# The expert loop of a hybrid encoder layer: silu's table load outside the loop, down's parts split at a slot's head, weight parts signalled in halves

## The chip, the cores and the metric

One core of a Trainium2 chip runs the whole kernel. The metric is the device time of one execution in microseconds (us). Times of this kernel are medians over several executions; a profile is one execution of its own, read by its span, which runs from the first to the last instruction.

## What is computed

The layer takes 1024 tokens of width 1024 in float32. It mixes them with two kinds of attention, then with attention over a memory of 256 tokens, and then routes them through 16 experts, of which each token uses two. The change touches only the last step:

```python
moe = jnp.zeros_like(t)
for e in range(N_EXPERTS):
    he = jax.nn.silu(t @ w_gate[e]) * (t @ w_up[e])
    moe = moe + gates[:, e:e + 1] * (he @ w_down[e])
h = h + moe.reshape(B, S, D)
```

`w_gate[e]` and `w_up[e]` are 1024 x 512, `w_down[e]` is 512 x 1024, all float32, 2 MB each.

## The kernel before

Each engine has an instruction stream of its own, written by hand, and they meet at semaphores (`wait_ge`, `then_inc`). The order of the work is the order in which each stream is written; no scheduler changes it.

**Slots.** Routing sorts the 2048 pairs of token and expert into slots of up to 128 rows of one expert. The number of slots depends on the data; in the run shown it is 24. Each engine runs one loop over them (`Fori(0, n_slots)`). An expert with more than 128 rows has two slots in a row; a table `newt` says for each slot whether its expert is another than the last one's.

**Split products.** A float32 product is made of three products of rounded parts: high x high, high x rest and rest x high (`split_product`, L1792). So each weight part must be split. ACT copies the loaded buffer `stage[part]` to `split[part][0]`, the high part (`high`, L1070), and DVE subtracts that from the loaded one, which gives the rest part (`rest`, L1455). Part 0 is gate, 1 is up, 2 is down. Each is split in four steps of 128 x 1024 elements (`PARTS = 4`), and ACT signals every step. The split is repeated in a slot that keeps its expert, but the load is skipped. There is one loaded buffer, one high and one rest buffer for each part.

**PE in slot s** (L2182 on). It multiplies the slot's rows by gate (24 matmuls into bank 2), then by up in two halves of the columns (24 + 24, banks 3 and 4), turns the first half of the product `hrow` (L2195), turns the rows of the next slot (`rows_in`, L2168), turns the second half of `hrow`, and multiplies by down (24 matmuls, banks 6 and 7). Before each weight part it waits with `weights` until DVE has signalled the whole rest part.

**ACT in slot s** (L1171 on). It waits for the gate product and applies silu (L1174), splits gate of the next slot, copies the turned `hrow` and the rows of the next slot (L1178, L1161), splits up of the next slot, waits for the down product and copies it out (L1186, the sum copies), and splits down of the next slot.

**DVE in slot s** (L1730 on). It does gate rest steps 0 and 1 of the next slot, then `hrow` = silu x share x up for the first half (L1737), gate step 2, `hrow` for the second half, the rest parts of `hrow` and of the next rows (L1744, L1719), gate step 3, and all of up and down of the next slot.

**SP** (L648 on) issues the loads. The load of a part for slot s + 2 waits until the rest of that part for slot s + 1 is done, and the order is gate, up, down. An issue whose expert stays moves nothing. **POOL** (L743 on) gathers the rows of a later slot once `rows_in` has emptied the buffer (L729), and adds the result rows to the output in HBM (L733) once ACT has copied them out.

Of the kernel before, what the change touches and what calls it, by code (L numbers as in the profile page):

```python
# [40 lines left out]
PARTS = 4  # L41
# [110 lines left out]
def moe_layer(nc, x, mem, positions, norm_mix_g, w_in, mla_q_norm_g, w_uq, mla_kv_norm_g, w_ukv,  # L152
# [18 lines left out]
    with ctx:  # L171
# [333 lines left out]
        def bank(i):  # L505
            return psum[:, i, :]
# [17 lines left out]
        def _(sp):  # L524
# [123 lines left out]
            def next_weights(s, parts, e, new):  # L648
                for part in parts:

                    sp.wait_ge(s_lo[part], s)
                    load(e, part, new > 0)
# [5 lines left out]
            next_weights(1, range(3), *plan(1))  # L658
            last = sp.snap(n_slots - 1)
            with sp.Fori(0, last) as s:  # L660
                e, new = plan(s + 2)
                next_weights(s + 2, range(3), e, new)
# [7 lines left out]
        def _(pool):  # L670
# [85 lines left out]
            all_split = pool.snap(n_slots + 1)  # L756
# [6 lines left out]
        def _(act):  # L763
# [298 lines left out]
            def high(s, part, used):  # L1062

                n = (DC if part < 2 else FC) // PARTS
                act.wait_ge(s_st[part], 16 * s + 16)
                if used is not None:
                    act.wait_ge(used, s)
                for c in range(PARTS):
                    k = slice(n * c, n * c + n)
                    act.activation(split[part][0][:, k, :], stage[part][:, k, :], ACT.Copy).then_inc(s_hi[part], 1)  # L1070
# [95 lines left out]
            high(0, 2, None)  # L1166
            act.wait_ge(s_ys, FIRST_ROWS)
            rows_high(0)
            act.wait_ge(s_plan, 1)
            n_slots = act.value_load(ends_i[0:1, NE - 1:NE], min_val=NE, max_val=SLOTS - 1)  # L1170
            with act.Fori(0, n_slots) as s:  # L1171

                act.wait_ge(s_gf, s + 1)
                act.activation(hrow, bank(2), ACT.Silu).then_inc(s_si, 1)  # L1174
                high(s + 1, 0, s_gf)
                for half in range(2):
                    act.wait_ge(s_ht, 2 * s + 1 + half)
                    act.activation(hTe[0][:, 2 * half:2 * half + 2, :].rearrange("p a b -> p (a b)"),  # L1178
                                   bank(5 - 2 * half)[:, 0:2 * P], ACT.Copy).then_inc(s_hth, 1)
                    if half == 0:  # L1180
                        rows_high(s + 1)
                high(s + 1, 1, s_ub)
                act.wait_ge(s_y, s + 1)
                act.wait_ge(s_yf, s + 1)
                for half in range(2):
                    act.activation(ysb[:, 512 * half:512 * half + 512], bank(6 + half), ACT.Copy).then_inc(s_yo, 1)  # L1186
                high(s + 1, 2, s_y)
# [3 lines left out]
        def _(dve):  # L1191
# [257 lines left out]
            def rest(s, part, steps):  # L1449

                n = (DC if part < 2 else FC) // PARTS
                for c in steps:
# [4 lines left out]
                    if c == PARTS - 1:  # L1457
                        ins.then_inc(s_lo[part], 1)
# [269 lines left out]
            rest(0, 2, range(PARTS))  # L1728
            n_slots = dve.value_load(ends_i[0:1, NE - 1:NE], min_val=NE, max_val=SLOTS - 1)
            with dve.Fori(0, n_slots) as s:  # L1730
                rest(s + 1, 0, (0, 1))
                for half, full in enumerate((s_ua, s_ub)):
                    cols = slice(256 * half, 256 * half + 256)
                    if half == 0:
                        dve.wait_ge(s_si, s + 1)
# [3 lines left out]
                    if half == 0:  # L1739
                        rest(s + 1, 0, (2,))  # L1740
# [7 lines left out]
                rest(s + 1, 0, (3,))  # L1748
                rest(s + 1, 1, range(PARTS))
                rest(s + 1, 2, range(PARTS))  # L1750
# [3 lines left out]
        def _(pe):  # L1754
# [416 lines left out]
            def weights(s, part):  # L2171

                pe.wait_ge(s_lo[part], s + 1)
# [8 lines left out]
            with pe.Fori(0, n_slots) as s:  # L2182
                pe.wait_ge(s_xl, 2 * s + 2)
                weights(s, 0)
                rows = lambda a, k: xT[a][:, k, :]
                split_product(bank(2), DC, rows, lambda b, k: split[0][b][:, k, :], s_gf)
                weights(s, 1)
                for half, full in enumerate((s_ua, s_ub)):
                    cols = slice(256 * half, 256 * half + 256)
                    split_product(bank(3 + half)[:, 0:256], DC, rows, lambda b, k: split[1][b][:, k, cols], full)  # L2190
# [8 lines left out]
                weights(s, 2)  # L2199
                for part in range(2):  # L2200
                    pe.wait_ge(s_htl, 2 * s + 1 + part)
# [33 lines left out]
```

## Time and profile before

| | us |
|---|---|
| median of 3 runs | 1583.45 |
| lowest and highest run | 1582.7, 1586.78 |
| the profiled execution's own time | 1585.15 |
| its span | 1583.4 |
| mean granted TensorE clock, share of full speed | 0.963 |

The page of the profile gives each engine's busy time as a share of the span. The windows give the same for chosen stretches. The list of waits groups idle time by the instruction that ended it. A timeline row has a start, a duration, the engine, the line and the operation with its output and inputs, how many instructions were merged, and in brackets how long the engine was idle before it and what released it. PEld is TensorE's loading of weights, which overlaps the matmuls. SPq is SP issuing a DMA.

### The profile page before, as it was taken

The page shows a single profiled execution, that of the slowest core. Times are in us where ns is not written, and L with a number is a line of the kernel's source. Part 1 is how long each engine was busy: PE and PEld are TensorE (multiplying, and loading weights), DVE is VectorE, ACT ScalarE, POOL GpSimd, SP SyncE. Part 2 cuts the span into 40 slices and gives each one's busy share as a digit, 9 for nine tenths or more (in the row PEclk, how much of TensorE's full clock was granted, in tenths as well). Part 3 has the DMA queues.
Part 4 walks back from the last instruction along what each step waited for, and adds up shares of the span by engine and source line. Part 5 has one row for each costly group of instructions (what it writes and reads, how often), then busy time and mean ns, then how long its engine had stood idle before and what let it go on. Part 6 is the DMA issues. An engine that isn't in the chain of part 4 may idle for free.

```text
span 1583.4 us, 20901 instructions
## 1 busy us (share of the span) xinstructions
PE 1453.7 (92%) x7417; PEld 1112.8 (70%) x7417; DVE 1030.1 (65%) x1900; ACT 925.7 (58%) x1624; POOL 167.5 (11%) x243
## 2 busy tenths in 40 slices
PE   6999999987889689999989999996999999999996
PEld 5888988444446444447868888885888888788885
DVE  4512126689759667757773333448888888888887
ACT  6320556676756545663333333343888888888886
POOL 0000000356610000000000000000111111111111
PEclk9999999999999789999989999996999999999998
DMA  6210215310020000102130100044996666666693
GB/s 213 57 34 8 96 68 213 143 47 1 1 107 1 1 1 28 54 27 84 50 120 1 54 28 27 28 160 161 372 360 215 202 207 204 202 205 212 212 366 102
DMA packets 87300, 184.81 MB, mean 117 GB/s; under 512 B 14273, under 2 KB 24513, under 8 KB 86465
## 3 DMA queue, kind: packets, MB, share of 16 engines
q1 hardware_dynamic: 77952, 161.90, 28.5%
q0 software_dynamic: 7200, 22.03, 5.4%
q8 instruction: 39, 0.64, 0.2%
q10 hardware_dynamic: 2080, 0.01, 0.1%
q14 instruction: 29, 0.23, 0.0%
HBM read 218.52 MB, written 26.21 MB: 155 GB/s over the span
## 4 chain that ended last, share of the span: by engine, by line
PE 63%; DMA 12%; DVE 9%; ACT 8%; issue 6%; POOL 1%; DVEq 0%; ACTq 0%; SPq 0%; POOLq 0%
PE psum L1792 21%; PE psum L2023 17%; DMA down_stage<-in_w_down 10%; PE psum L1776 7%; PE psum L1919 6%; PE psum L1940 4%; PE psum L1769 3%; PE psum L1906 3%; DVE down_rest L1455 3%; ACT down_high L1070 2%; POOL arena L709 1%; DVE gate_rest L1455 1%; DVE mx L1418 1%; PE psum L2072 1%; ACT L1174 1%
## 5 line engine op out<-in xcount | busy, mean ns | idle before, releaser
L1919 PE MATMUL psum<-arena 64*128 64x512 f32 (+7 forms) x384 | 124.1, 545 | 20.6 <-ACT arena L1041 12.0
L1455 DVE TENSOR_TENSOR gate_rest<-gate_stage,gate_high 128x1024 fp32r<-128x1024 f32 x100 | 119.8, 1220 | 31.3 <-ACT gate_high L1070 31.3
L1455 DVE TENSOR_TENSOR down_rest<-down_stage,down_high 128x1024 fp32r<-128x1024 f32 x100 | 115.8, 1220 | 31.1 <-ACT down_high L1070 31.1
L1919 PEld LDWEIGHTS psum<-arena 64*128 64x128 f32 (+1 forms) x384 | 50.2, 196 | 102.0 <-issue 46.9
L1455 DVE TENSOR_TENSOR up_rest<-up_stage,up_high 128x1024 fp32r<-128x1024 f32 x100 | 115.8, 1220 | 7.7 <-ACT up_high L1070 7.5
L1776 PE MATMUL psum<-arena 128*128 128x512 f32 (+2 forms) x352 | 119.2, 491 | 0.8 <-DVE arena L1361 0.8
L1940 PEld LDWEIGHTS psum<-ident,arena 128*128 128x128 f32 x576 | 70.8, 152 | 66.6 <-ACT arena L774 32.7
L774 ACT ACTIVATE arena<-psum 128x512 f32<-128x512 f32 (+1 forms) x192 | 85.8, 501 | 49.2 <-PE psum L1940 49.1
L1940 PE MATMUL psum<-ident,arena 128*128 128x128 f32 x576 | 93.6, 302 | 20.4 <-DVE arena L1377 14.3
L1792 PE MATMUL psum<-up_rest,rows_high 128*128 128x256 f32 x384 | 108.7, 283 | 0.0
L1070 ACT ACTIVATE up_high<-up_stage 128x1024 fp32r<-128x1024 f32 x100 | 97.5, 1049 | 19.0 <-DMA up_stage<-in_w_up 19.0
L1792 PE MATMUL psum<-up_high,rows_rest 128*128 128x256 f32 x384 | 108.6, 283 | 0.0
L1792 PE MATMUL psum<-up_high,rows_high 128*128 128x256 f32 x384 | 108.5, 283 | 0.0
L1369 DVE TENSOR_TENSOR_SCAN arena<-arena,singles 128x768 f32<-128x768 f32 (+7 forms) x64 | 90.9, 1420 | 27.0 <-POOL arena L709 26.9
L1070 ACT ACTIVATE down_high<-down_stage 128x1024 fp32r<-128x1024 f32 x100 | 97.6, 1053 | 17.0 <-DMA down_stage<-in_w_down 17.0
L709 POOL TENSOR_SCALAR_AFFINE_SELECT arena<-arena 128x128 f32<-128x128 f32 x128 | 94.5, 760 | 76.2 <-ACT arena L946 69.7
L1769 PE MATMUL psum<-ident,arena 128*128 128x128 f32 (+1 forms) x520 | 75.1, 287 | 28.9 <-ACT arena L791 12.5
L1070 ACT ACTIVATE gate_high<-gate_stage 128x1024 fp32r<-128x1024 f32 x100 | 97.3, 1048 | 5.4 <-DMA gate_stage<-in_w_gate 5.2
L1776 PEld LDWEIGHTS psum<-arena 128*128 128x128 f32 x352 | 66.0, 193 | 43.1 <-issue 26.7
L1769 PEld LDWEIGHTS psum<-ident,arena 128*128 128x128 f32 (+1 forms) x520 | 62.2, 143 | 44.6 <-issue 21.6
L1906 PE MATMUL psum<-arena 128*64 128x512 f32 (+3 forms) x384 | 84.8, 521 | 1.8 <-ACT arena L774 1.8
L1792 PE MATMUL psum<-down_high,hidden_high 128*128 128x512 f32 x192 | 77.6, 404 | 0.0
(362 smaller groups left out, 3649.0 us busy)
## 6 DMA issues: line engine op xcount, KB each, us to landing
gate_stage<-in_w_gate SPq DMA_DIRECT2D x25, 2048.0 KB
up_stage<-in_w_up SPq DMA_DIRECT2D x25, 2048.0 KB
down_stage<-in_w_down SPq DMA_DIRECT2D x25, 2048.0 KB
arena<-in_x SPq DMA_DIRECT2D x16, 512.0 KB, 3.6
arena<-in_w_mkv SPq DMA_DIRECT2D x8, 1024.0 KB, 6.2
arena<-in_w_in SPq DMA_DIRECT2D x4, 1024.0 KB, 10.1
arena<-in_w_mo SPq DMA_DIRECT2D x4, 1024.0 KB, 6.5
mv_times_w_mo_spill<-arena SPq DMA_DIRECT2D x8, 512.0 KB, 2.8
```

The costliest lines, as they stand in the source:

```text
L709: pool.affine_select(out=block_, in_=block_, compare_op=ALU.is_gt, fill=fill, base=0, pattern=[[-1, P]], channel_multiplier=1).then_inc(ma ...
L774: do(act.activation(dst, src, ACT.Copy), s_te["act"])
L1070: act.activation(split[part][0][:, k, :], stage[part][:, k, :], ACT.Copy).then_inc(s_hi[part], 1)
L1369: one(dve.tensor_tensor_scan(fall[:, a, SEQ - L:SEQ][:, ::-1], f_sb[:, n % 3, 0:L][:, ::-1], tiny.to_broadcast([P, L]), 1.0, ALU.mult, ALU ...
L1455: ins = dve.tensor_tensor(split[part][1][:, k, :], stage[part][:, k, :], split[part][0][:, k, :].bitcast(F32), ALU.subtract)
L1769: mm = pe.transpose(dst[0:rows, at:at + P], src, ident[:, :])
L1776: mm = pe.matmul(dst, a, b, start=(i == 0), stop=(i == n - 1))
L1792: mm = pe.matmul(dst, lhs(a, k), rhs(b, k), start=(k == 0 and i == 0), stop=(k == n - 1 and i == 2))
L1906: pe.matmul(bank(6 + u % 2)[HD * a:HD * a + HD, lo:512], value(p, a, j), bufs[:, k % 4, lo:512], start=(j == 0), stop=(j == GRP * g + 3)). ...
L1919: mm = pe.matmul(pair(1 + a)[:, at:end], lhs, rhs(at, end), start=True, stop=True)
L1940: mm = pe.transpose(dst[:, r * P:(r + 1) * P], rows(u, r, a)[:, j * P:(j + 1) * P], ident[:, :])
L2023: mm = pe.matmul(dst, lhs[a][:, k, :], w[b][:, k, cols], start=(k == ks[0] and k % n == 0 and i == 0), stop=(k % n == n - 1 and i == 2))
```

## The change

Before the loop ACT applies silu to one column, and no longer splits down for slot 0; nor does DVE. In the loop:

- ACT splits down of the present slot right behind silu, gate of the next slot behind the hidden and row parts, then step 0 of up, then the two sum copies, then up's steps 1 to 3.
- DVE does down step 0, the first half of `hrow`, down steps 1 and 2, the second half, the parts of `hrow` and rows, down step 3, and then all of gate and up of the next slot.
- DVE signals a rest part after its second and its fourth step, so that each count is double. PE waits for the first half before the first half of a product's matmuls and for the second half before the others. The number and order of the matmuls stay.
- SP issues down of slot s + 1 once down of slot s is split, and then gate and up of slot s + 2. The table of experts is read twice in an iteration.

```diff
@@ -645,21 +645,24 @@
             sp.wait_ge(s_plan, 1)
             n_slots = sp.value_load(ends_i[0:1, NE - 1:NE], min_val=NE, max_val=SLOTS - 1)
 
-            def next_weights(s, parts, e, new):
-                for part in parts:
-
-                    sp.wait_ge(s_lo[part], s)
-                    load(e, part, new > 0)
+            def next_weights(part, rests_done, e, new):
+                sp.wait_ge(s_lo[part], rests_done)
+                load(e, part, new > 0)
 
             def plan(s):
                 return (sp.value_load(eidt[0:1, bass.ds(s, 1)], min_val=0, max_val=NE - 1),
                         sp.value_load(newt[0:1, bass.ds(s, 1)], min_val=0, max_val=1))
 
-            next_weights(1, range(3), *plan(1))
+            e, new = plan(1)
+            for part in range(2):
+                next_weights(part, 2, e, new)
             last = sp.snap(n_slots - 1)
             with sp.Fori(0, last) as s:
+                e, new = plan(s + 1)
+                next_weights(2, 2 * s + 2, e, new)
                 e, new = plan(s + 2)
-                next_weights(s + 2, range(3), e, new)
+                for part in range(2):
+                    next_weights(part, 2 * s + 4, e, new)
             all_added = sp.snap(16 * n_slots)
             sp.wait_ge(s_ya, all_added)
             sp.sem_inc(s_end, 1)
@@ -753,7 +756,7 @@
                 pool.wait_ge(s_ya, 16 * s + 16)
                 pool.sem_inc(s_yf, 1)
             all_fetched = pool.snap(16 * n_slots + 32)
-            all_split = pool.snap(n_slots + 1)
+            all_split = pool.snap(2 * n_slots + 2)
             for part in range(2):
                 pool.wait_ge(s_lo[part], all_split)
             pool.wait_ge(s_xg, all_fetched)
@@ -1059,13 +1062,13 @@
                                   ACT.Square, scale=DM ** -0.5, accum_out=to), sem_)
                 do.settle()
 
-            def high(s, part, used):
+            def high(s, part, used, steps=range(PARTS)):
 
                 n = (DC if part < 2 else FC) // PARTS
                 act.wait_ge(s_st[part], 16 * s + 16)
                 if used is not None:
                     act.wait_ge(used, s)
-                for c in range(PARTS):
+                for c in steps:
                     k = slice(n * c, n * c + n)
                     act.activation(split[part][0][:, k, :], stage[part][:, k, :], ACT.Copy).then_inc(s_hi[part], 1)
 
@@ -1163,28 +1166,30 @@
 
             act.wait_ge(s_mop, T)
             high(0, 1, None)
-            high(0, 2, None)
             act.wait_ge(s_ys, FIRST_ROWS)
             rows_high(0)
+
+            do(act.activation(m4[:, 0:1], m4[:, 0:1], ACT.Silu))
             act.wait_ge(s_plan, 1)
             n_slots = act.value_load(ends_i[0:1, NE - 1:NE], min_val=NE, max_val=SLOTS - 1)
             with act.Fori(0, n_slots) as s:
 
                 act.wait_ge(s_gf, s + 1)
                 act.activation(hrow, bank(2), ACT.Silu).then_inc(s_si, 1)
-                high(s + 1, 0, s_gf)
+                high(s, 2, None)
                 for half in range(2):
                     act.wait_ge(s_ht, 2 * s + 1 + half)
                     act.activation(hTe[0][:, 2 * half:2 * half + 2, :].rearrange("p a b -> p (a b)"),
                                    bank(5 - 2 * half)[:, 0:2 * P], ACT.Copy).then_inc(s_hth, 1)
                     if half == 0:
                         rows_high(s + 1)
-                high(s + 1, 1, s_ub)
+                high(s + 1, 0, s_gf)
+                high(s + 1, 1, s_ub, (0,))
                 act.wait_ge(s_y, s + 1)
                 act.wait_ge(s_yf, s + 1)
                 for half in range(2):
                     act.activation(ysb[:, 512 * half:512 * half + 512], bank(6 + half), ACT.Copy).then_inc(s_yo, 1)
-                high(s + 1, 2, s_y)
+                high(s + 1, 1, None, (1, 2, 3))
 
 
         @block.vector
@@ -1454,7 +1459,7 @@
                     dve.wait_ge(s_hi[part], PARTS * s + c + 1)
                     ins = dve.tensor_tensor(split[part][1][:, k, :], stage[part][:, k, :],
                                             split[part][0][:, k, :].bitcast(F32), ALU.subtract)
-                    if c == PARTS - 1:
+                    if c % 2:
                         ins.then_inc(s_lo[part], 1)
 
             def tile_of(j):
@@ -1725,19 +1730,16 @@
             one(dve.tensor_copy(share, bank(7)[:, 0:TAB]))
             one(dve.tensor_tensor(share, share, bank(7)[:, TAB:2 * TAB], ALU.add))
             rest(0, 1, (1, 2, 3))
-            rest(0, 2, range(PARTS))
             n_slots = dve.value_load(ends_i[0:1, NE - 1:NE], min_val=NE, max_val=SLOTS - 1)
             with dve.Fori(0, n_slots) as s:
-                rest(s + 1, 0, (0, 1))
                 for half, full in enumerate((s_ua, s_ub)):
                     cols = slice(256 * half, 256 * half + 256)
+                    rest(s, 2, (1, 2) if half else (0,))
                     if half == 0:
                         dve.wait_ge(s_si, s + 1)
                     dve.wait_ge(full, s + 1)
                     dve.scalar_tensor_tensor(out=hrow[:, cols], in0=hrow[:, cols], scalar=share[:, bass.ds(s, 1)],
                                              in1=bank(3 + half)[:, 0:256], op0=ALU.mult, op1=ALU.mult).then_inc(s_h, 1)
-                    if half == 0:
-                        rest(s + 1, 0, (2,))
                 for half in range(2):
                     v = slice(2 * half, 2 * half + 2)
                     dve.wait_ge(s_hth, 2 * s + 1 + half)
@@ -1745,9 +1747,9 @@
                                       hTe[0][:, v, :].bitcast(F32), ALU.subtract).then_inc(s_htl, 1)
                     if half == 0:
                         rows_rest(s + 1)
-                rest(s + 1, 0, (3,))
+                rest(s, 2, (3,))
+                rest(s + 1, 0, range(PARTS))
                 rest(s + 1, 1, range(PARTS))
-                rest(s + 1, 2, range(PARTS))
 
 
         @block.tensor
@@ -2168,9 +2170,9 @@
                         mm = pe.transpose(bank(half)[:, c * P:(c + 1) * P], xg[:, at:at + P], ident[:, :])
                     mm.then_inc(s_xt, 1)
 
-            def weights(s, part):
-
-                pe.wait_ge(s_lo[part], s + 1)
+            def weights(s, part, half):
+
+                pe.wait_ge(s_lo[part], 2 * s + half + 1)
 
             pe.wait_ge(s_sh, 1)
             share_table(range(10))
@@ -2181,13 +2183,18 @@
             n_slots = pe.value_load(ends_i[0:1, NE - 1:NE], min_val=NE, max_val=SLOTS - 1)
             with pe.Fori(0, n_slots) as s:
                 pe.wait_ge(s_xl, 2 * s + 2)
-                weights(s, 0)
                 rows = lambda a, k: xT[a][:, k, :]
-                split_product(bank(2), DC, rows, lambda b, k: split[0][b][:, k, :], s_gf)
-                weights(s, 1)
+                for part in range(2):
+                    weights(s, 0, part)
+                    split_product(bank(2), DC, rows, lambda b, k: split[0][b][:, k, :], s_gf if part else None,
+                                  range(4 * part, 4 * part + 4))
                 for half, full in enumerate((s_ua, s_ub)):
                     cols = slice(256 * half, 256 * half + 256)
-                    split_product(bank(3 + half)[:, 0:256], DC, rows, lambda b, k: split[1][b][:, k, cols], full)
+                    for part in range(2):
+                        if half == 0:
+                            weights(s, 1, part)
+                        split_product(bank(3 + half)[:, 0:256], DC, rows, lambda b, k: split[1][b][:, k, cols],
+                                      full if part else None, range(4 * part, 4 * part + 4))
                 for half in range(2):
                     pe.wait_ge(s_h, 2 * s + 1 + half)
                     for c in range(2):
@@ -2196,8 +2203,8 @@
                     mm.then_inc(s_ht, 1)
                     if half == 0:
                         rows_in(s + 1)
-                weights(s, 2)
                 for part in range(2):
+                    weights(s, 2, part)
                     pe.wait_ge(s_htl, 2 * s + 1 + part)
                     for half in range(2):
                         split_product(bank(6 + half), FC, lambda a, k: hTe[a][:, k, :],
```

In the order of the built program the head of ACT's loop stood like this (the row `arena<-psum` at L1174 is silu):

```order
L1171 ISA
L1174 ACT_TABLE_LOAD
L1174 ACTIVATE arena<-psum 128x512
L1065 ISA
L1070 ACTIVATE gate_high<-gate_stage 128x1024 x4
```

and now, from just ahead of the loop (L1175 is its head, and silu is at L1178):

```order
L1164 ACTIVATE rows_high<-psum 128x512 x2
L1172 ACT_TABLE_LOAD
L1172 ACTIVATE m<-m 128x1
L1174 TENSOR_LOAD ends_i
L1174 ISA x2
L1175 UNCONDITIONAL_BRANCH
L1175 ISA
L1178 ACTIVATE arena<-psum 128x512
L1068 ISA
L1073 ACTIVATE down_high<-down_stage 128x1024 x4
```

The table load stands ahead of the loop, and down's high steps follow silu where gate's did.

The end of ACT's loop before, from the second hidden part on (`arena<-psum` x2 are the sum copies):

```order
L1178 ACTIVATE hidden_high<-psum 128x256
L1070 ACTIVATE up_high<-up_stage 128x1024 x4
L1186 ACTIVATE arena<-psum 128x512 x2
L1070 ACTIVATE down_high<-down_stage 128x1024 x4
L1171 REGISTER_ALU
```

and now:

```order
L1182 ACTIVATE hidden_high<-psum 128x256
L1068 ISA
L1073 ACTIVATE gate_high<-gate_stage 128x1024 x4
L1073 ACTIVATE up_high<-up_stage 128x1024
L1191 ACTIVATE arena<-psum 128x512 x2
L1073 ACTIVATE up_high<-up_stage 128x1024 x3
L1175 REGISTER_ALU
```

Gate's four steps and one of up's stand ahead of the sum copies now, and up's other three behind them.

The end of DVE's loop before, from the second hidden rest part on:

```order
L1744 TENSOR_TENSOR hidden_rest<-psum,hidden_high 128x256
L1454 REGISTER_ALU
L1455 TENSOR_TENSOR gate_rest<-gate_stage,gate_high 128x1024
L1455 TENSOR_TENSOR up_rest<-up_stage,up_high 128x1024 x4
L1455 TENSOR_TENSOR down_rest<-down_stage,down_high 128x1024 x4
```

and now:

```order
L1746 TENSOR_TENSOR hidden_rest<-psum,hidden_high 128x256
L1459 REGISTER_ALU
L1460 TENSOR_TENSOR down_rest<-down_stage,down_high 128x1024
L1459 ISA
L1460 TENSOR_TENSOR gate_rest<-gate_stage,gate_high 128x1024
L1459 REGISTER_ALU
L1460 TENSOR_TENSOR gate_rest<-gate_stage,gate_high 128x1024
L1459 REGISTER_ALU
L1460 TENSOR_TENSOR gate_rest<-gate_stage,gate_high 128x1024
L1459 REGISTER_ALU
L1460 TENSOR_TENSOR gate_rest<-gate_stage,gate_high 128x1024
L1460 TENSOR_TENSOR up_rest<-up_stage,up_high 128x1024 x4
```

Five steps stand between the hidden rest part and up's steps, where one stood.

## Rows read from the trace of the kernel before

**Rows 1.** The page, busy us of each engine, share of the span, instructions.

```profile
PE 1453.7 (92%) x7417; PEld 1112.8 (70%) x7417; DVE 1030.1 (65%) x1900; ACT 925.7 (58%) x1624; POOL 167.5 (11%) x243
```

**Rows 2.** Windows of the expert loop: length, busy us, clock, DMA share, GB/s.

```profile
1100.92:1120.91 19.99, 19.99 (x108) 17.26 (x109) 18.57 (x21) 10.76 (x14) 1.15 (x2) 0.92 1.00 371
1120.91:1218.56 97.65, 93.14 (x542) 80.56 (x540) 82.86 (x91) 81.53 (x100) 13.93 (x15) 1.00 0.88 305
1218.56:1530.53 311.97, 298.14 (x1729) 257.69 (x1728) 264.31 (x289) 259.63 (x320) 44.41 (x48) 1.00 0.67 225
1530.53:1569.65 39.12, 37.66 (x217) 32.04 (x215) 33.15 (x37) 32.72 (x40) 5.55 (x6) 1.00 0.61 204
1257.81:1276.18 18.37, 18.37 (x109) 16.10 (x108) 15.57 (x18) 15.56 (x20) 2.77 (x3) 1.00 1.03 355
1276.18:1296.46 20.28, 18.75 (x110) 16.11 (x108) 17.49 (x20) 16.81 (x21) 2.78 (x3) 1.00 0.26 71
```

**Rows 3.** Waits in the loop: us in total, times, longest us.

```profile
PEld psum L2195 <- DVE arena L1737: 27.1, 33, 2.8
PE psum L2195 <- DVE arena L1737: 19.6, 29, 2.6
...
PE psum L1792 <- DVE rows_rest L1719: 0.4, 1, 0.4
...
ACT up_high L1070 <- DMA up_stage<-in_w_up: 19.0, 12, 2.0
```

**Rows 4.** Timeline of PE, the slot from 1257.81, and the next one's wait.

```profile
1263.29 0.28 PE L1792 MATMUL psum<-up_high,rows_high 128*128 128x256 f32 x1
...
1269.04 0.38 PE L2195 MATMUL psum<-ident,arena 128*128 128x128 f32 x2
...
1270.53 0.47 PE L1792 MATMUL psum<-down_high,hidden_high 128*128 128x512 f32 x1
...
1288.85 0.44 PE L2195 MATMUL psum<-ident,arena 128*128 128x128 f32 x2 [1.32 <-DVE arena L1737]
```

**Rows 5.** Timeline of ACT over the same two slots.

```profile
1272.90 3.91 ACT L1070 ACTIVATE up_high<-up_stage 128x1024 fp32r<-128x1024 f32 x4 [1.64 <-DMA up_stage<-in_w_up]
...
1279.25 3.90 ACT L1070 ACTIVATE down_high<-down_stage 128x1024 fp32r<-128x1024 f32 x4 [1.47 <-DMA down_stage<-in_w_down]
1283.17 1.28 ACT L1174 ACT_TABLE_LOAD   x1
1284.47 0.60 ACT L1174 ACTIVATE arena<-psum 128x512 f32<-128x512 f32 x1
```

**Rows 6.** Timeline of SP, issues of loads.

```profile
1109.20 0.37 SPq L539 DMA_DIRECT2D down_stage<-in_w_down  x1
...
1254.99 0.39 SPq L539 DMA_DIRECT2D gate_stage<-in_w_gate  x1
1259.22 0.38 SPq L539 DMA_DIRECT2D up_stage<-in_w_up  x1
...
1273.61 0.09 SPq L539 DMA_DIRECT2D gate_stage<-in_w_gate  x1
```

**Rows 7.** Timeline of DVE, the end of the row parts in the slot from 1257.81.

```profile
1271.73 0.41 DVE L1744 TENSOR_TENSOR hidden_rest<-psum,hidden_high 128x256 fp32r<-128x256 f32 x1
1272.07 1.22 DVE L1455 TENSOR_TENSOR gate_rest<-gate_stage,gate_high 128x1024 fp32r<-128x1024 f32 x1
1273.99 4.63 DVE L1455 TENSOR_TENSOR up_rest<-up_stage,up_high 128x1024 fp32r<-128x1024 f32 x4 [0.71 <-ACT up_high L1070]
```

**Rows 8.** Timeline of POOL, the issue of the adding DMA.

```profile
1260.00 1.59 POOL L733 DMA_INDIRECT layer_out<-arena,idx  x1 [6.31 <-ACT arena L1186]
```

**Rows 9.** Windows of DMA while gate, up and down land (columns as Rows 2).

```profile
1258.00:1265.00 7.00, 7.00 (x39) 6.02 (x39) 5.83 (x6) 6.96 (x9) 1.59 (x1) 1.00 1.02 363
1265.00:1269.00 4.00, 4.00 (x36) 4.00 (x35) 3.23 (x4) 3.58 (x4) 0.00 (x0) 1.00 1.04 244
...
1276.00:1278.00 2.00, 2.00 (x11) 1.65 (x9) 2.00 (x3) 1.78 (x3) 0.00 (x0) 1.00 0.92 365
```

## The prediction

> **What bounds the kernel now.** The page comes first. PE is busy 92% of the span and DVE 65%, but those are averages over stages with different limits [rows 1]. The change touches only the expert loop, so the table of windows is cut at its slots [rows 2]. The loop runs from 1100.92 to 1569.65 us, 468.7 us in 24 slots. A slot in which PE never waits takes 18.37 us, 1257.81 to 1276.18, with PE busy through all of it. The next one takes 20.28. Both are the same 24 gate, 48 up and 24 down matmuls, so every slot above 18.37 holds a wait (the first also runs at a granted clock of 0.92). The three stretches after it hold 97.65 - 5 x 18.37 = 5.8 us, 311.97 - 16 x 18.37 = 18.1 us and 39.12 - 2 x 18.37 = 2.4 us of excess, 26.3 us in all. That is the most that any reordering here can bring.
>
> The list of waits says where the excess sits [rows 3]: PE's weight loads wait 27.1 us for DVE's product `hrow` before its transposes (L2195), the matmuls themselves 19.6 us. That list has one other wait of PE in the loop, 0.4 us, and none for weight parts, so signalling parts in halves has nothing to win by itself. PE's timeline shows one such wait, 1.32 us at 1288.85 [rows 4]. Why `hrow` is late stands in ACT's timeline [rows 5]. In the slot before, `up_high` waits 1.64 us for its load, then `down_high` 1.47 us; after it come the table load, 1.28 us, and silu only at 1284.47. DVE does two gate steps and the product behind that. So DMA is late first and the table load makes it worse. DMA's share agrees [rows 2]: 1.03 at 355 GB/s in the slot from 1257.81, 0.26 in the next. SP's issues show why [rows 6]: an issue of 0.38 us is a real load, one of 0.09 is skipped because the expert stays. The first six slots each need a new expert, then every second, and both of the last two.
>
> **The change, part by part.** The sum is made against the profiled execution, 1585.15 us with a span of 1583.4. The median of the runs, 1583.45, is 1.7 lower, and I add the difference to it.
>
> The table load leaves the loop: 24 x 1.28 = 31 us less on ACT. The one that stays runs before the first gate product ends, while ACT waits: 0. It shortens the path only where ACT was late, 12 slots by the waits on up's load [rows 3], so at most 15 us, and only if nothing else is late there. The trace has silu 0.02 us behind the end of the load (1283.17 + 1.28, [rows 5]). The Trainium skill (ScalarE: Activation LUTs, section What ACT_TABLE_LOAD costs) adds 1.38 us of drain to a load. By the page those 12 slots would hold up to 17 us more for this cut; the trace shows no such gap, and the sum goes without it.
>
> ACT and DVE get the same weight work in another order. I lay a slot out from T, the start of its gate product, with the free slot's T = 1257.81. PE starts up at T+5.48, the transposes at T+11.23, down at T+12.72 [rows 4]. ACT: silu at T+5.7, four down steps of 0.96 (a group of four takes 3.90, [rows 5]) to T+10.0, the hidden and row parts behind the transposes, four gate steps from about T+13.7, up step 0 from T+17.5, the two sum copies, up steps 1 to 3 to T+22.5. It is free before the next silu at T+24.0. DVE's row parts end at T+14.3, where `gate_rest` follows now [rows 7]. With 1.135 a step (a group of four takes 4.63) down step 3 ends at T+15.5, the gate steps at T+20.0, the up steps at T+24.5. PE wants the second half of down at T+12.72+2.83 = T+15.55, up's two halves at T+23.85 and T+25.3. So without late loads a slot stays at 18.37, but one margin is under 0.1 us. The waits on halves are needed in this order: a whole gate part, ready at T+20.0 against T+18.37, would hold every slot 1.6 us.
>
> Loads move, since each waits for the rest steps that free its buffer. After the row parts DVE had one gate step to do, and a gate issue followed at 1273.61 = T+15.8 [rows 6]. Now one down and four gate steps stand there, four more, 4.5 us: T+20.3, which is 1.9 after the next T, where it was 2.8 before it (1254.99). Up goes by the same 4.5 from T+1.4 (1259.22) to about T+6.4, down to T+15.8. SP's two extra table reads and its new down wait stand between down's and gate's rest steps, 4.5 us apart, and cost nothing. Gate's high part moves from T+6.9 to T+13.7, further than its load. Up's moves from about T+13.1 to T+17.5, only as far as its load.
>
> So up's landing decides. From gate's issue to up's landing it took 17.9 us (1254.99 to 1272.90, [rows 5, 6]). In that DMA moved the two loads at 363 GB/s, and the added rows, whose DMA POOL issues at T+2.2, cut the rate to 244 GB/s for 4 us [rows 8, 9]. That issue stays at T+2.2, inside. The gather of the next rows fell into down's time before, around 1276 to 1278; now the end of up's load stands there. For it the floor is nothing and the ceiling is the 2 us of that window; I take 1.4, since down, which met it, was the load that ended there. Up lands at T + 1.9 + 17.9 + 1.4 = T+21.2, bounds T+19.8 and T+21.8.
>
> What PE loses from a landing at u: step 0 takes 0.96 and the sum copies 0.98, so step 1 ends at u+3.0. DVE then runs three steps of 1.135 and signals the last half at u+6.5. PE wants it at T+25.3. Above u = T+18.8 it waits one for one: 2.4 us at T+21.2, 1.0 and 3.0 at the bounds. Before, such a pair of slots lost 18.1/8 = 2.26. The wait changes its place, from the transposes to the up product, and hardly its size.
>
> Sum by stretch [rows 2]. First slot: 0. Slots 2 to 6: DMA carries an expert a slot, 371 GB/s at share 1.00 while it does, and the bytes stay. Down's second load goes some 9 us later (1109.20 to about 1118.3, the first T + 15.8 and the 1.6 us by which that slot is slow), a hole in DMA that the first slots' early loads mostly cover: +0.5, bounds -2 and +3. Slots 7 to 22: 8 x (2.4 - 2.26) = +1.1, bounds -10 and +6. Last two, both with new experts: +0.9, bounds -1 and +2. After the last product stand the same copies and the same adding DMA: 0. The sum is +2.5 us: **1583.45 + 2.5 = 1586.0**. A measurement of this kernel can tell 0.3%, 4.75 us, from no change, so this is a forecast of no change.
>
> **Rivals.**
> **A, the loads are covered, faster.** If up lands by T+18.8, the 18.1 us of slots 7 to 22 go: 1583.45 - 18 = 1565.5. At the lower bound of the landing 10 go: 1573.5. For it: DMA has a slot at share 0.26 behind each busy one, down's load now starts late and alone, and ACT has 1.28 us more. Against: the 17.9 us held only two loads and the adding DMA, with share 1.02 and 1.04 through it [rows 9]. 24 in 100.
>
> The Trainium skill (DMA: Bandwidth & Descriptors, section Bandwidth) measures 425 GB/s for the largest transfers. By that two loads of 2.1 MB take 1.6 us less than at 363 GB/s, up lands near T+19.6 and the time is about 1572. Rows 9 do not bear it out for gate and up.
>
> **B, the load falls deeper, slower.** Gather and adding DMA both fall wholly on up, and late sum copies push the next adding DMA into the following load. The point is u = T+21.5: there a pair loses 2.7, and 8 x 0.44 + 1.4 passes 4.75. Typical is u = T+22.1, 3.3 a pair: 8 x 1.04 + 1.4 = +9.7, 1593. For it: my landing is 0.3 us under that point, and the hole in the first slots. Against: the loads of the sole new expert have the next slot free. 22 in 100.
>
> **C, DVE becomes the bound, slower.** Down's last half has under 0.1 us to spare, and DVE's loop gets more register instructions and signals. From 0.2 us a slot on (24 x 0.2 = 4.8) it decides; at 0.3 it gives 1590.6. For it: DVE is busy 17.49 of 20.28 already [rows 2]. Against: register work stands before gate's step at 1272.07 too, and it starts 0.34 us after an operation of 0.41 [rows 7], without a gap. 12 in 100.
>
> That the edit does not do what it says is nearly excluded: in the printed order the table load stands before the loop, the weights in the new order, and the loads behind the waits named.
>
> **How the numbers follow.** Forecast 42, A 24, B 22, C 12. Of the 42, 41 lie within 4.75 us and 1 above it, so faster 0.24, same 0.41, slower 0.22 + 0.12 + 0.01 = 0.35. The range reaches from A's price at the landing's lower bound to just above B's: 1573 to 1596. It leaves out the better half of A, about 12 in 100, and 6 above.
>
> **What the next profile would show.** Right: no ACT_TABLE_LOAD between silus; PE's wait at L2195 mostly gone, and waits of 2 to 2.5 us before up's matmuls on DVE `up_rest`, in every second slot; ACT's `up_high` waiting 3 us and more for its load; gate loads issued near T+1.9; a free slot still 18.37. Wrong: nearly all slots at 18.4 (A); up landing after T+21.5 in the loading slots (B); or PE waiting for `down_rest` in slots with and without loads (C).

## The result and the profile after

| | before | changed |
|---|---|---|
| median, us | 1583.1 (4 runs) | 1568.65 (4 runs) |
| lowest and highest | 1582.7, 1586.78 | 1566.76, 1571.85 |
| span of the profiled execution | 1583.4 | 1567.7 |
| the expert loop in it, first gate to last down matmul | 468.60 | 454.35 |

The ratio is 0.9906, 95% interval 0.9883 to 0.9928. The kernel is 14.4 us faster, where the forecast was +2.5 us. The fall lies wholly in the loop, 14.25 us. The loop's start moves from profile to profile by some us with nothing changed ahead of it (1098.6 to 1104.5 over the kernels below), so the loop's own length is the finer measure, and it is given for each experiment. Here and below it is cut 0.13 us ahead of the last matmul's end; [rows 2] go to the end, where the same loop is 468.7.

The page of the changed kernel, against [rows 1]: ACT is 35 us less busy, PE and DVE are within 3 us. POOL shows 15 us more, but with ACT's copies moved (below) it is at 167.5 again, as before, while the time stays.

```profile
PE 1450.9 (93%) x7417; PEld 1109.4 (71%) x7417; DVE 1028.8 (66%) x1896; ACT 890.8 (57%) x1598; POOL 182.1 (12%) x243
```

The windows of its loop, cut at the same slots as [rows 2] and with the same columns (length, busy us of PE, PEld, DVE, ACT, POOL, clock, DMA share, GB/s); the last two rows are one slot that issues loads of gate and up and the slot behind it:

```profile
1099.61:1119.44 19.83, 19.83 (x108) 17.14 (x109) 14.17 (x17) 11.50 (x16) 1.16 (x2) 0.93 0.77 271
1119.44:1217.84 98.40, 94.19 (x541) 80.07 (x540) 83.49 (x91) 74.65 (x95) 16.84 (x15) 1.00 0.93 323
1217.84:1514.18 296.34, 296.14 (x1730) 256.94 (x1728) 266.37 (x289) 237.63 (x303) 54.33 (x48) 1.00 0.69 230
1514.18:1553.96 39.78, 37.68 (x217) 31.84 (x215) 33.61 (x37) 30.53 (x39) 5.55 (x6) 1.00 0.76 257
1254.77:1273.20 18.43, 18.43 (x109) 16.04 (x108) 16.67 (x19) 13.93 (x18) 3.97 (x3) 1.00 0.84 265
1273.20:1291.74 18.54, 18.54 (x110) 16.08 (x108) 16.61 (x19) 15.85 (x20) 2.78 (x3) 1.00 0.45 166
```

Slots 2 to 6 went from 97.65 to 98.40 us, the last two from 39.12 to 39.91 (with the 0.13 us of the last matmul). All of the gain, 15.6 us, is in slots 7 to 22, from 311.97 to 296.34. There PE is busy through 296.14 of 296.34. The slot behind a load takes 18.54 instead of 20.28.

The list of waits in that loop (total us, times, longest us), against [rows 3]:

```profile
ACT up_high L1073 <- DMA up_stage<-in_w_up: 23.6, 14, 2.8
...
PE psum L1794 <- DVE up_rest L1460: 5.7, 9, 1.0
...
PE psum L2202 <- DVE arena L1741: 0.5, 1, 0.5
```

PE's wait for `hrow`, 19.6 us, is down to 0.5. A wait for up's rest part came in its place, as forecast, but of 5.7 us in 9 waits, not 2.4 in every loading pair. The timelines of SP and POOL in the slot from 1254.77 show when the loads are issued and when the rows' DMAs are, and that of ACT shows when up has landed, against [rows 5, 6, 8]:

```profile
1256.69 0.39 SPq L539 DMA_DIRECT2D gate_stage<-in_w_gate  x1
1260.93 0.38 SPq L539 DMA_DIRECT2D up_stage<-in_w_up  x1
1270.57 0.38 SPq L539 DMA_DIRECT2D down_stage<-in_w_down  x1
```

```profile
1256.96 2.00 POOL L736 DMA_INDIRECT layer_out<-arena,idx  x1 [5.94 <-ACT arena L1191]
1268.33 0.18 POOL L729 COPY idx<-idx_all 128x2 int32 x1 [9.36 <-DMA layer_out<-arena,idx]
1269.32 1.79 POOL L732 DMA_INDIRECT arena<-tn_rows,idx  x1 [0.81 <-POOL idx L729]
```

```profile
1273.58 1.06 ACT L1073 ACTIVATE up_high<-up_stage 128x1024 fp32r<-128x1024 f32 x1 [1.48 <-DMA up_stage<-in_w_up]
1274.54 1.07 ACT L1191 ACTIVATE arena<-psum 128x512 f32<-128x512 f32 x2
```

Gate's load goes at T+1.9, up's at T+6.2, down's at T+15.8, gate's and down's where the prediction put them and up's 0.2 us sooner. Up has landed at 1273.58 - 1254.77 = T+18.8. From gate's issue to there it took 16.9 us, not 17.9 + 1.4. Over the eight pairs it was 16.8 to 17.1 us.

### The profile page after: what moved, and what is told of

The parts are those of the page before. It is cut to its first block, busy times and chain, and to the rows that moved or that the text cites. A ratio compares the mean times of both kernels' runs of the same rounds, so it can differ in the third digit from the quotient of the medians.

```text
span 1567.7 us, 21242 instructions
## 1 busy us (share of the span) xinstructions
PE 1450.9 (93%) x7417; PEld 1109.4 (71%) x7417; DVE 1028.8 (66%) x1896; ACT 890.8 (57%) x1598; POOL 182.1 (12%) x243
## 4 chain that ended last, share of the span: by engine, by line
PE 71%; DVE 9%; DMA 8%; ACT 5%; issue 4%; POOL 1%; DVEq 0%; ACTq 0%; SPq 0%; POOLq 0%
PE psum L1794 28%; PE psum L2025 17%; DMA up_stage<-in_w_up 8%; PE psum L1778 8%; PE psum L1921 6%; PE psum L1942 4%; PE psum L1771 3%; PE psum L1908 3%; DVE up_rest L1460 3%; POOL arena L712 1%; DVE gate_rest L1460 1%; DVE mx L1423 1%; PE psum L2074 1%; PE psum L2170 1%; ACT gate_high L1073 1%
## 5 line engine op out<-in xcount | busy, mean ns | idle before, releaser
L1460 DVE TENSOR_TENSOR up_rest<-up_stage,up_high 128x1024 fp32r<-128x1024 f32 x100 | 117.0, 1219 | 15.9 <-ACT up_high L1073 15.6
L1460 DVE TENSOR_TENSOR gate_rest<-gate_stage,gate_high 128x1024 fp32r<-128x1024 f32 x100 | 115.6, 1216 | 1.2 <-ACT gate_high L1073 1.2
L1771 PE MATMUL psum<-ident,arena 128*128 128x128 f32 (+1 forms) x520 | 74.8, 286 | 29.1 <-ACT arena L794 12.7
L1073 ACT ACTIVATE down_high<-down_stage 128x1024 fp32r<-128x1024 f32 x96 | 93.6, 1049 | 10.1 <-DMA down_stage<-in_w_down 10.1
L1794 PEld LDWEIGHTS psum<-up_high,rows_high 128*128 128x128 f32 x384 | 73.5, 191 | 11.2 <-DVE up_rest L1460 10.0
```

What stands on the lines that cost most here:

```text
L1460: ins = dve.tensor_tensor(split[part][1][:, k, :], stage[part][:, k, :], split[part][0][:, k, :].bitcast(F32), ALU.subtract)
L1771: mm = pe.transpose(dst[0:rows, at:at + P], src, ident[:, :])
L1794: mm = pe.matmul(dst, lhs(a, k), rhs(b, k), start=(k == 0 and i == 0), stop=(k == n - 1 and i == 2))
```

## The experiments

Two questions stand. Which part of the change brought the gain: silu's table load outside the loop (theory T), or the order of splits and loads (theory O)? And why did up land 2.4 us earlier than worked out?

**Silu alone.** The kernel before, plus the line ahead of the loop:

```diff
             rows_high(0)
+            do(act.activation(m4[:, 0:1], m4[:, 0:1], ACT.Silu))
             act.wait_ge(s_plan, 1)
```

> The kernel before with silu's table load outside the loop and nothing else. Theory T (table load): in the 12 or so slots in which ACT was late the load of 1.28 us stood on the path, so this alone takes most of the measured 14.4 us: -10 to -15 us. Theory O (order and timing of the loads): down's load still lands late and ACT, DVE and the product behind it stay in the same order, so at most -4 us. The forecast had set this term at most 15 us and then let it go.

Median 1573.1 us, ratio to before 0.9948 (0.9927 to 0.9968), some 9.7 us faster. The window of its whole loop:

```profile
1099.34:1556.98 457.64, 448.19 (x2592) 387.68 (x2592) 398.19 (x435) 354.70 (x452) 65.16 (x71) 1.00 0.74 252
```

The loop is 11.0 us shorter than before. Theory O's bound of 4 us has fallen: the table load did stand on the path.

**The order alone.** The changed kernel without that line, so that the table load is in the loop again:

```diff
             rows_high(0)
-            do(act.activation(m4[:, 0:1], m4[:, 0:1], ACT.Silu))
             act.wait_ge(s_plan, 1)
```

> The changed kernel without the silu ahead of the loop, so that the table load is back in it. Theory T: +10 us or more, almost back to the kernel before. Theory O: ACT has 1.55 us before silu in a slot that loads and 0.44 us in the one behind it, so 0.84 us of 1.28 shows on ACT in every second slot and part of that is taken up by DVE: 0 to +7 us over the changed kernel.

Median 1571.66 us, ratio 0.9922 (0.9907 to 0.9938). That is 3 us above the changed kernel, but not in the loop; its loop began at 1104.53. The window of its loop and ACT's timeline around two silus, the first in a slot that issues loads:

```profile
1104.53:1558.67 454.14, 447.74 (x2592) 385.91 (x2592) 396.63 (x431) 382.82 (x475) 78.55 (x71) 1.00 0.75 254
```

```profile
1264.36 1.28 ACT L1176 ACT_TABLE_LOAD   x1
1265.90 0.60 ACT L1176 ACTIVATE arena<-psum 128x512 f32<-128x512 f32 x1 [0.25 <-PE psum L1792]
...
1283.97 1.28 ACT L1176 ACT_TABLE_LOAD   x1
1285.27 0.60 ACT L1176 ACTIVATE arena<-psum 128x512 f32<-128x512 f32 x1
```

454.14 us: as short as the changed kernel's 454.35. In the new order, in a slot that issues loads, the table load runs in time in which ACT waits for the gate product. In the slot behind, which starts at 1278.64, silu comes at T+6.6 where the changed kernel has it at T+5.7. Down's split follows at T+7.1 instead of T+6.8, since in the changed kernel it waits there for down's load, so only 0.3 us of the 0.9 is left, and the loop shows no loss. So theory T's +10 has fallen as well. The two parts remove the same wait: either alone takes 11.0 or 14.5 us out of the loop, both together 14.25. They don't add.

**Whole parts.** The changed kernel, with PE waiting for all of a part:

```diff
-                pe.wait_ge(s_lo[part], 2 * s + half + 1)
+                pe.wait_ge(s_lo[part], 2 * s + 2)
```

> The changed kernel, PE waiting for the whole rest part before the first half of each product. By the layout of a slot the gate part is whole at T+20.0 against T+18.4, so each slot gets 1.6 us longer, and up adds nothing behind that: +38 us, with PE waiting for gate_rest in every slot. The rival is that halves matter as little as before: within 3 us.

Median 1660.95 us, ratio 1.0486: 92 us above the changed kernel, more than double of what was expected, and at another part. PE's list of waits, the matmul behind one of them, and the windows of the stretch before and of the down product behind it:

```profile
PE psum L1794 <- DVE down_rest L1460: 64.8, 23, 2.8
PE psum L1794 <- DVE up_rest L1460: 4.5, 23, 0.2
```

```profile
1325.18 0.50 PE L1794 MATMUL psum<-down_high,hidden_high 128*128 128x512 f32 x1 [2.82 <-DVE down_rest L1460]
```

```profile
1309.23:1325.18 15.95, 12.96 (x85) 11.39 (x83) 11.13 (x14) 12.13 (x17) 2.78 (x3) 1.00 0.20 63
1325.18:1332.42 7.24, 7.24 (x25) 5.75 (x25) 5.62 (x5) 2.65 (x3) 0.00 (x0) 0.76 0.35 89
```

PE waits for down, whose last quarter DVE ends at about T+15.5, while PE is ready at T+12.7. The expectation had looked at gate only. The clock adds to it (below, under the hardware). In this order the signals in halves are worth 90 us.

**Halves alone.** The kernel before with `if c % 2` in place of `if c == PARTS - 1` at DVE's signal, the counts doubled, and PE's waits by halves as in the change.

> The kernel before with rest parts signalled and waited for in halves and nothing else. PE had no wait for a weight part, so both theories expect no change: within 2 us of before.

Median 1582.17 us, ratio 0.9996 (0.9983 to 1.0008), loop 467.11 us. As expected: halves bring nothing where nobody waits for a part.

**No loads.** Both kernels with the table that says where an expert changes set to "never":

```diff
-            do(dve.tensor_tensor(newt[:, 1:SLOTS], junk[:, 513:512 + SLOTS], junk[:, 512:511 + SLOTS], ALU.not_equal))
+            do(dve.tensor_tensor(newt[:, 1:SLOTS], junk[:, 513:512 + SLOTS], junk[:, 512:511 + SLOTS], ALU.is_lt))
```

> The changed kernel with every load after slot 0's skipped (the table says that no expert changes; the products use the first expert's weights). Every slot should fall to the free slot of 18.37 us: the loop from 454.5 to about 442.3 us, so -12 us against the changed kernel and -26 us against before. If DVE's order had a price of its own (the rival that DVE becomes the bound), slots would stay above 18.4.

> The kernel before with the same loads skipped. If late loads are the only root and the table load hurts only behind them, each slot falls to 18.37 us and this takes as long as the changed kernel without loads: -26 us against before. If the table load costs time by itself, it stays above that by up to 1.28 us a slot, 30 us.

Medians 1557.88 and 1560.21 us; the loops are equal within 0.1 us, and the second profile's begins 4.1 us later. The loop of the changed kernel, then that of the one before:

```profile
1099.93:1542.51 442.58, 442.58 (x2592) 385.87 (x2592) 397.46 (x431) 351.76 (x453) 74.74 (x71) 1.00 0.22 48
```

```profile
1104.03:1546.71 442.68, 442.68 (x2592) 387.45 (x2592) 399.22 (x435) 380.35 (x474) 65.15 (x71) 1.00 0.22 48
```

Both orders run at 18.37 us a slot with PE busy throughout, the second with its table load in each slot. So all 26 us of excess before, and all 12 now, come with the loads, and neither the table load nor DVE's order (rival C) costs anything by itself.

**The gather.** Both kernels with the loop's gather bounded to row 0. In `fetch` a bound is handed to the DMA (`bounds_check=0, oob_is_err=False`), and in the loop it is set (cut to that line):

```diff
-                fetch(idx[:, 0:1])
+                fetch(idx[:, 0:1], 0)
```

Rows of real tokens then don't move. The padding of a slot does: its index is 0 (`ALU.max` with 0, L1694), which the bound lets through.

> The kernel before with the loop's gather of rows bounded so that nearly no row moves (slots work on old rows). The forecast took 17.9 us from gate's issue to up's landing as two loads and the adding DMA, and added 1.4 for the gather. If the gather of the slot before was already inside those 17.9, here it is 16.5 to 17.2. If it was not, it stays 17.9.

> The changed kernel with the same bound on the gather. If the gather now runs behind up's load, the time from gate's issue to up's landing stays at 16.9 us and the loop changes by under 2 us in the pairs. If it still costs up something, it falls.

One run each, 1562.54 and 1567.0 us. In the kernel before without the gather, the issue of gate, ACT's wait for up behind it, and the window of the loop:

```profile
1247.90 0.39 SPq L539 DMA_DIRECT2D gate_stage<-in_w_gate  x1
```

```profile
1264.96 3.91 ACT L1071 ACTIVATE up_high<-up_stage 128x1024 fp32r<-128x1024 f32 x4 [1.05 <-DMA up_stage<-in_w_up]
```

```profile
1100.24:1547.64 447.40, 444.51 (x2592) 387.43 (x2592) 398.83 (x435) 383.41 (x474) 66.51 (x71) 1.00 0.70 241
```

17.1 us from issue to landing instead of 17.9, and a loop of 447.40 instead of 468.60. In the changed kernel without it the same time is 1270.45 - 1253.61 = 16.8 us, against 16.9 with it, and the loop is 451.47 against 454.35. The single slot understates it. Over the eight pairs, from gate's issue to ACT's first step of up, which waits for the landing in each of them:

| us | gate's issue to up's landing: range, mean | slots 7 to 22 |
|---|---|---|
| before | 17.8 to 19.6, 18.25 | 311.97 |
| before, gather bounded | 16.8 to 17.3, 17.0 | 297.09 |
| changed | 16.8 to 17.1, 17.0 | 296.34 |
| changed, gather bounded | 16.8 to 17.2, 17.0 | 296.68 |

```profile
1213.76:1510.85 297.09, 295.40 (x1730) 257.64 (x1728) 264.38 (x289) 259.23 (x320) 45.39 (x48) 1.00 0.64 218
1214.67:1511.35 296.68, 296.36 (x1729) 257.08 (x1728) 266.53 (x289) 238.23 (x304) 54.64 (x48) 1.00 0.64 212
```

So the gather cost the old order 14.9 us in these slots and costs the new order none there; the 2.9 us that the changed kernel gains by the bound lie in slots 2 to 6 (95.02 for 98.40). And it is above all the gather in front of gate's load that counts. The pairs have two gathers. With the bound the one ahead of gate's issue at 1247.90 moves next to nothing, and the one on the end of down's load, which is mostly padding, still moves 0.48 of its 0.52 MB; in the other pairs it moves 0.16 to 0.48. These are the rows of POOL's DMA queue in 1247.3 to 1248.3 and in 1268 to 1271 (packets, MB, share of the 16 engines):

```profile
q0 software_dynamic: 144, 0.00, 8.7%
```

```profile
q0 software_dynamic: 144, 0.48, 39.8%
```

The traces with the whole gather say where it stood. The kernel before, POOL and the DMA window around gate's issue at 1254.99:

```profile
1252.69 1.00 POOL L729 DMA_INDIRECT arena<-tn_rows,idx  x1 [0.81 <-POOL idx L726]
```

```profile
1254.00:1257.00 3.00, 3.00 (x15) 2.41 (x14) 3.00 (x4) 2.36 (x3) 0.00 (x0) 1.00 0.73 186
```

DMA carries the gather at 186 GB/s until 1257, just where gate's load starts; the next one comes at 1276 to 1278, on the end of down's. In the changed kernel the gather has ended at 1254.1, and gate is issued at 1256.69. The window behind gate's issue is empty of rows, and so is the one in which up lands:

```profile
1256.00:1259.00 3.00, 3.00 (x15) 2.48 (x14) 3.00 (x4) 2.89 (x4) 2.00 (x1) 1.00 0.30 32
1258.00:1262.00 4.00, 4.00 (x26) 3.61 (x25) 2.90 (x3) 2.44 (x4) 0.97 (x1) 1.00 0.86 284
1262.00:1267.00 5.00, 5.00 (x45) 5.00 (x44) 4.57 (x6) 3.36 (x5) 0.00 (x0) 1.00 1.00 261
1267.00:1273.00 6.00, 6.00 (x29) 4.63 (x28) 5.77 (x8) 5.09 (x7) 1.97 (x2) 1.00 1.04 394
```

Only 1262 to 1267, at 261 GB/s, holds other traffic, the adding DMA. The next gather is issued at 1269.32, and its rows move from 1273.5 on, about 4 us later, just behind up's end.

**No adding.** The changed kernel with `bounds_check=0` at the adding DMA.

> The changed kernel with the adding DMA bounded so that nearly no row is added (the output lacks the experts' sum). DMA then moves some 8 MB less. If up's landing is set by what DMA carries between gate's issue and it, up lands 2 to 3 us sooner after gate's issue, 14 to 15 us instead of 16.9, and the 8 pairs fall to 2 x 18.37. If the first and last slots are bound by DMA's bytes, their excess of 6.5 and 2.6 us falls as well, together -5 to -9 us against the changed kernel. If the excess there is latency, under -3 us.

Median 1559.04 us. The loop:

```profile
1100.68:1547.27 446.59, 443.92 (x2592) 386.13 (x2592) 394.66 (x431) 353.15 (x453) 89.41 (x71) 1.00 0.68 241
```

It is 7.8 us shorter, and by the landings in the trace up is there 13.9 us after gate's issue, 3.0 less. Slots 2 to 6 take 5.1 us less and the last two 2.9, most of their excess, so by the terms of the expectation those are bound by bytes. The pairs did not fall to 2 x 18.37, as was expected:

```profile
1213.80:1510.40 296.60, 294.99 (x1730) 256.84 (x1728) 264.70 (x289) 236.85 (x303) 62.97 (x48) 1.00 0.61 213
```

296.60 us for slots 7 to 22, against 296.34. Up is there in time in each of them, and the excess is now in slots in which ACT waits for down's load, up to 1.5 us (slots 8 and 18 take 19.3 and 19.2). Why down lands later there is open.

**A load in every slot.** The changed kernel with the table of new experts set to "always" (`ALU.is_ge`).

> The changed kernel loading an expert in every slot. If such slots are bound by what DMA can carry (6.3 MB of weights and about 1 MB of rows at 360 to 370 GB/s), every slot takes 19.6 to 20.0 us: +18 to +24 us over the changed kernel, with DMA's share at 1.00. If they are bound by the chain of load, split and next load, DMA's share stays under 0.95 and slots take over 20.

Median 1599.77 us, 31 us above the changed kernel, more than expected. The loop:

```profile
1099.17:1583.73 484.56, 452.43 (x2592) 385.53 (x2592) 397.23 (x431) 352.51 (x453) 71.23 (x71) 1.00 0.99 351
```

DMA's share is 0.99, so bytes bind. 23 slots take 20.2 us each, at 351 GB/s 7.1 MB a slot. The rate was taken too high, not the rule.

**Copies first, and a later load.** Two changes of the new order. In one, ACT's sum copies stand ahead of all of up:

```diff
-                high(s + 1, 1, s_ub, (0,))
...
-                high(s + 1, 1, None, (1, 2, 3))
+                high(s + 1, 1, s_ub)
```

> The changed kernel with the two sum copies ahead of all four of up's high steps. In a slot that loads, up lands at T+18.8 and the down product ends at T+18.6, so the copies fit while ACT waits for the load, and up's steps 1 to 3 come 0.8 us sooner: the 0.15 us behind each loading slot goes, and some of the excess of the first six: -1 to -4 us against the changed kernel. The rival (DVE is last there, not ACT) expects no change.

Median 1570.1 us, ratio to before 0.9913 (0.9896 to 0.993), loop 454.99 us: no change from the changed kernel, which is what the rival expects; whether DVE is last there was not looked at. In a pair, about 0.1 us moved from the slot behind to the loading slot.

In the other, SP issues up's load only after two of ACT's next down steps:

```diff
+                sp.wait_ge(s_hi[2], PARTS * s + PARTS + 2)
                 next_weights(1, 2 * s + 4, e, new)
```

> The changed kernel with up's load issued only when the third down high step of the slot is next, about 2 us later (SP waits for two of ACT's down steps). If up's landing sits at the edge and PE loses one for one behind it, each of the 8 pairs loses 1.8 us and the first and last slots about 6 us together: +18 to +24 us over the changed kernel. If there is slack behind it, under +5 us.

Median 1572.17 us, ratio 0.9926, loop 459.03 us: +4.7, not +18, and 3.7 of the 4.7 are two slots (20.3 and 20.5) in which down landed late. SP's and ACT's timelines show why up costs so little, for a slot that starts at 1260.91:

```profile
1262.64 0.39 SPq L539 DMA_DIRECT2D gate_stage<-in_w_gate  x1
1269.08 0.38 SPq L539 DMA_DIRECT2D up_stage<-in_w_up  x1
```

```profile
1279.93 1.06 ACT L1074 ACTIVATE up_high<-up_stage 128x1024 fp32r<-128x1024 f32 x1 [1.82 <-DMA up_stage<-in_w_up]
```

Issued 2.0 us later in its slot, up lands at T+19.0, 0.2 later. From 1266 to 1270, across up's issue, DMA's share is 1.06, so an earlier issue would have found DMA busy with gate's load, and what counts is when DMA has carried both. The slot behind took 18.80 us.

## Why the prediction was wrong

Point by point, by its own steps:

- **What bounds the kernel**: right. Without loads both kernels run at 18.37 us a slot; all of the 26 us came with the loads.
- **The table load**: right that it only counts behind a late load, and its ceiling of 15 us held; alone it brings 11.0 us in the loop. It was then dropped because another wait, 2.4 us a pair for up, would take its place. That it is worth nothing in this order is so, the loop is 454 us with or without it, but that reason was not: the wait for up is 0.2 to 0.4 us a pair, and the table load fits into time that ACT has.
- **The order, and the issue times of loads**: right to 0.2 us (T+1.9, T+6.2, T+15.8), though for up T+1.4 and 4.5 make T+5.9 and not the T+6.4 of the text. Down's last quarter was in time, so rival C fell. The count of what halves save named gate and 1.6 us; it was down, 2.8 us, though the layout of the same paragraph has down whole at T+15.5 and wanted at T+12.72.
- **Up's landing, the step that failed.** The text took 17.9 us from gate's issue to up's landing as "the two loads at 363 GB/s, and the added rows", and added 1.4 for the gather. Measured: 16.8 to 17.1, and 0. The 17.9 already held the tail of the slot before's gather, which stood in front of gate's load: with that gather out of the way the same stretch is 17.0 in the old order too, against a mean of 18.25. The move of gate's issue by 4.7 us against the slot took it out of the gather's way. The text did not see it because [rows 9] begin at 1258.00, 3 us behind gate's issue at 1254.99; its "share 1.02 and 1.04 through it" covers 11 of the 17.9 us. And the 1.4 was put on up though [rows 9] had the gather at 1276 to 1278, which is T+18.2 to T+20.2, behind all but the end of an up that lands at T+18.8. So the gather was counted twice, once in the measured stretch and once beside it. Up landed at T+18.8 and not at T+21.2.
- **What a late landing costs**: right. The threshold was put at T+18.8, and landings of T+18.8 to T+19.1 cost 0.2 to 0.4 us a pair, where the rule gives up to 0.3. For slot 6 up landed 1.7 us into the slot, which cost 1.5; the rule, by which the first 0.4 us are free, gives 1.3. With 18.8 put in, the pairs lose 0 instead of 2.26: 8 x 2.26 = 18, and 15.6 were measured.
- **The other stretches**: +0.5 for slots 2 to 6 was +0.75, +0.9 for the last two was +0.8, and the first slot took 0.2 less.

So rival A came true, between its two prices (1565.5 and 1573.5), and against the argument made there, "the 17.9 us held only two loads and the adding DMA". The bound of T+19.8 was no bound, as it was made from the same 17.9; the range missed the result for that, though the text itself gave about 12 in 100 to the better half of A.

The traces have 394 GB/s over the 6 us in which up lands in the changed kernel, and 351 over the loop that loads always. In the kernel before DMA carries only the end of up's load and the start of down's from 1271 to 1275, and is faster:

```profile
1271.00:1275.00 4.00, 4.00 (x18) 3.23 (x18) 3.29 (x5) 2.36 (x4) 1.00 (x1) 1.00 1.04 417
```

The forecast set the 425 GB/s of the Trainium skill (DMA: Bandwidth & Descriptors, section Bandwidth) aside for gate and up. Over the stretches in which they land that holds, with 363 and 394 GB/s; the four us above come within 2% of the page's figure. With T+19.6, which the forecast worked out from the page, its own rule gives 1573.2 and not "about 1572".

## What to carry to other kernels

A measured latency holds whatever shared the channel in it. Before it is moved to another place in time, list what DMA carried in that stretch from a microsecond or two ahead of the issue on, and lay each of these transfers out on the new time line; a small transfer just in front of a large one counts. Two edits that remove the same wait are to be priced together, since here 11.0 and 14.5 us made 14.25. And where a slot's layout fits to a tenth, signals in halves are worth what they replace, here 90 us, and nothing in a layout in which nobody waits.

## What was not expected of the hardware

In the kernel with whole parts PE stands still for 2.8 us ahead of down, and in 15 of the 23 later slots the granted clock then falls: 0.76 over the down product, the first of it at half of full speed (1.2 of 2.4 GHz), so that the product takes 7.24 us instead of 5.69. That is 1.55 us more behind the wait. In the other eight the same wait of 2.8 us is followed by a clock of 1.00, so the wait alone does not decide it. In the kernel before, whose longest wait is 2.6 us at L2195, the clock stayed at 1.00 through the loop behind the first slot. That a gather of 0.5 MB in front of a load costs 14.9 us over 16 slots in one order and nothing in the other was not expected either.
